# A two-block transformer kernel on one core: a reordered head, ten convolution taps shared with ScalarE, and the second gate computed on VectorE

## What is computed

```
mod_x = silu(c) @ w_ada + b_ada          # 6144 columns: sh1 sc1 g1 sh2 sc2 g2
hx = modulate(rms_norm(x), sh1, sc1);  hc = modulate(rms_norm(ctx), csh1, csc1)
q, k, v, u = split(hx @ w_in);  kc, vc = hc @ w_in[:, 512:1536]
attn = neighbourhood_attention(rope(q), q, rope(k), v, kc, vc, rpb)
a, b = split(u);  h = a * sigmoid(b)
h = depthwise_conv(h, dw_kernel, 31 taps, 512 channels) + dw_bias
conv = silu(layer_norm(h))
x = x + g1 * (concat(attn, conv) @ w_out)
x = x + g2 * (square(relu(modulate(rms_norm(x), sh2, sc2) @ w_mlp1)) @ w_mlp2)
```

## Time and profile before

| | us |
|---|---|
| median of 3 runs | 737.4 |
| lowest and highest | 736.58, 737.42 |
| the profiled execution's own time | 736.31 |
| its span, first to last instruction | 734.5 |
| PE busy | 722.9 (98%) |
| DVE busy | 508.9 (69%) |
| ACT busy | 398.0 (54%) |

### The profile page before, as it was taken

How to read it: one execution, slowest core, us unless ns; L and a number is a source line. 1 busy time by engine, 2 the same in 40 slices (tenths; PEclk the granted TensorE clock), 3 DMA queues, 4 the chain that set the end, 5 groups by cost and what they waited for, 6 DMA issues and landing times.

```text
span 734.5 us, 9784 instructions
## 1 busy us (share of the span) xinstructions
PE 722.9 (98%) x3824; PEld 578.6 (79%) x3824; DVE 508.9 (69%) x924; ACT 398.0 (54%) x662; POOL 25.0 (3%) x44
## 2 busy tenths in 40 slices
PE   8989999999999999999999999999999999999996
PEld 7668885568888888888878777778888888888885
DVE  4678999889667555565988799865857445544544
ACT  3366337886666545556545677666466344334432
POOL 1030012000100000000010000000000000000000
PEclk9999999999999999999999999999999999999999
DMA  9993939945464655445538533344366555655511
GB/s 365 415 354 117 374 112 360 368 161 176 159 223 158 229 192 209 172 163 182 159 101 302 200 115 115 117 176 167 114 230 205 195 175 188 209 175 172 172 58 57
DMA packets 73741, 144.90 MB, mean 197 GB/s; under 512 B 4112, under 2 KB 27664, under 8 KB 72672
## 3 DMA queue, kind: packets, MB, share of 16 engines
q1 hardware_dynamic: 71888, 138.98, 54.6%
q0 software_dynamic: 1520, 5.03, 1.9%
q10 hardware_dynamic: 288, 0.27, 0.1%
HBM read 143.22 MB, written 1.05 MB: 196 GB/s over the span
## 4 chain that ended last, share of the span: by engine, by line
PE 93%; DVE 3%; issue 2%; ACT 1%; POOL 1%; POOLq 0%; DVEq 0%
PE bank L414 22%; PE bank L416 22%; PE bank L415 22%; PE bank L735 5%; PE bank L396 5%; PE bank L733 3%; PE bank L433 2%; PE bank L476 1%; PE bank L454 1%; PE bank L577 1%; PE bank L490 1%; DVE WL L1480 1%; PE bank L599 1%; PE bank L852 1%; PE bank L874 1%
## 5 line engine op out<-in xcount | busy, mean ns | idle before, releaser
L1480 DVE TENSOR_TENSOR WL<-W,WH 128x1024 fp32r<-128x1024 f32 (+2 forms) x222 | 249.5, 1169 | 48.8 <-ACT WH L1005 48.5
L1005 ACT ACTIVATE WH<-W 128x1024 fp32r<-128x1024 f32 (+2 forms) x222 | 211.7, 1011 | 52.9 <-DMA W<-in_w_mlp 40.5
L414 PE MATMUL bank<-WH,AHL 128*128 128x512 f32 (+1 forms) x480 | 189.2, 394 | 2.3 <-DVE WL L1480 2.0
L416 PE MATMUL bank<-WH,AHL 128*128 128x512 f32 (+1 forms) x480 | 185.4, 386 | 0.0
L415 PE MATMUL bank<-WL,AHL 128*128 128x512 f32 (+1 forms) x480 | 185.2, 386 | 0.0
L414 PEld LDWEIGHTS bank<-WH,AHL 128*128 128x128 f32 x480 | 90.2, 188 | 24.0 <-DVE WL L1480 3.5
L416 PEld LDWEIGHTS bank<-WH,AHL 128*128 128x128 f32 x480 | 90.1, 188 | 18.7
L415 PEld LDWEIGHTS bank<-WL,AHL 128*128 128x128 f32 x480 | 90.3, 188 | 16.8
L414 PE MATMUL bank<-WH,HH 128*128 128x512 f32 (+1 forms) x218 | 84.9, 390 | 0.0
L416 PE MATMUL bank<-WH,HL 128*128 128x512 f32 (+1 forms) x218 | 84.5, 388 | 0.0
L415 PE MATMUL bank<-WL,HH 128*128 128x512 f32 (+1 forms) x218 | 84.4, 387 | 0.0
(11 more groups left out here) (265 smaller groups left out, 831.4 us busy)
## 6 DMA issues: line engine op xcount, KB each, us to landing
W<-in_w_mlp SPq DMA_DIRECT2D x32, 1024.0 KB, 5.5
W<-in_w_in SPq DMA_DIRECT2D x24, 1024.0 KB, 5.1
W<-in_w_ada SPq DMA_DIRECT2D x12, 1024.0 KB, 8.0
WX<-in_w_ada SPq DMA_DIRECT2D x12, 1024.0 KB, 9.9
W<-in_w_gate SPq DMA_DIRECT2D x22, 512.0 KB, 4.2
W<-in_w_up SPq DMA_DIRECT2D x22, 512.0 KB, 5.3
W<-in_w_down SPq DMA_DIRECT2D x11, 1024.0 KB, 5.0
W<-in_w_out SPq DMA_DIRECT2D x8, 1024.0 KB, 5.1
```

Of the source, the lines that this page charges most:

```text
L414: e.matmul(po, hs, wh[:, k, c0:c0 + cw], start=first and k == 0, stop=False)
L416: ins = e.matmul(po, ls, wh[:, k, c0:c0 + cw], start=False, stop=last and k == unit.nk - 1)
L1005: e.activation(m.WH[unit.slot][:, c], m.W32[unit.slot][:, c], ACT.Copy).then_inc(S["w_hi"], 1)
L1480: e.tensor_tensor(m.WL[unit.slot][:, c], m.W32[unit.slot][:, c], m.WH[unit.slot][:, c].bitcast(F32), ALU.subtract).then_inc(S["w_lo"], 1)
```

## The change

It reorders the head, moves ten of the thirty-one taps to another form, and takes g2 out of the attention.

1. **Head.** 11 matmuls on ones instead of 16 ahead of `mod_first(0)`, and none instead of 4 ahead of `mod_turn(0)`. The context is loaded two units earlier, ahead of the eighth block's two tiles. ACT squares it after block 5 instead of after block 7, and DVE normalises its first half after block 6 and its second half between the two k units. ACT's table load for the sigmoid moves ahead of block 7, both sigmoids of b behind the k units' WH. Slots 3 and 12 change places in the first 16 entries, so that k's first unit waits for block 5's tile and not for block 6's.
2. **Ten taps.** For taps 21 to 30, ACT writes the product hp * tap into one of two buffers (`tap_products`, 4 instructions of 128x256 for each tap), and DVE adds it to cacc in one instruction of 128x1024 (`add_product`). DVE keeps 80 of its 120 tap instructions; 60 of them and all ten additions stand before the attention. The buffers lie where V and U are, so ACT's copy of V waits for all ten additions.
3. **g2.** Four `w_ada` units of 1 MB, `mod_second` steps 12 to 15, two tails and two of four `rows2_lo` go. Instead SP loads the same 1024x1024 columns as rows in four pieces of 1 MB after the loads of m2 units 2 to 5, DVE sums them over rows (8 instructions of 128x1024) in chunks 2 to 5, ACT and DVE split the sum, and PE adds over partitions with four matmuls of 512 columns (`gate_sum`) in chunk 6.

The core of the diff:

```diff
-    slots = [2, 4, 3, 5, 12, 0, 13, 1, 2, 4, 3, 5, 12, 0, 13, 1, 2, 3, 4, 5, 0, 1]
+    slots = [2, 4, 12, 5, 3, 0, 13, 1, 2, 4, 12, 5, 3, 0, 13, 1, 2, 3, 4, 5, 0, 1]
...
+    def gate_rows(n):                                  # SP
+        w.wait_ge(S["out_mm"], 8)
+        if n > 1:
+            w.wait_ge(S["g2"], 2 * n - 2)
...
-    for n in range(16):
+    for n in range(14):
         load(n)
     e.dma_start(m.XC[:, :, :], ...)
-    for n in range(16, len(units)):
+    for n in range(14, len(units)):
         load(n)
+        if n in gate_at:
+            gate_rows(gate_at.index(n))
...
-    keep_busy(16)                                      # PE
+    keep_busy(11)
     mod_first(0)
-    keep_busy(4)
     mod_turn(0)
     keep_busy(8)
...
+    def gate_sum():
+        w.wait_ge(S["comb_r"], 2)
+        w.wait_ge(S["g2_hi"], 1)
+        w.wait_ge(S["g2"], 9)
+        for n in range(2):
+            cs = slice(512 * n, 512 * n + 512)
+            take(4 + n)
+            e.matmul(bank[4 + n][:, :], m.onesR[:, :].to_broadcast([128, 128]), m.gH[:, cs], start=True, stop=False)
+            e.matmul(bank[4 + n][:, :], m.onesR[:, :].to_broadcast([128, 128]), m.gL[:, cs], start=False,
+                     stop=True).then_inc(S["g2_mm"], 1)
+            frees(4 + n, ("g2", n + 10))
...
-        mod_second(2 * u)                              # PE, attention step u
-        if u:
-            mod_second_tail(u - 1)
+        if u < 4:
+            mod_second(2 * u)
+        if u in (1, 2, 3, 4, 6):
+            mod_second_tail(min(u - 1, 4))
...
-        mod_second(2 * u + 1)
+        mod_second(2 * u + 1 if u < 4 else u + 4)
...
-    for k in range(8):                                 # ACT, head
+    for k in range(6):
         hi()
         high_x(k)
     w.wait_ge(S["l_xc"], 16)
     for tb in range(2):
         square(2 + tb, m.XC[:, tb, :], m.XC2[:, tb, :])
     hi()
+    high_x(6)
     e.activation(m.stat[:, 92:93], m.stat[:, 94:95], ACT.Sigmoid)
+    hi()
+    high_x(7)
+    hi(2)
...
+    def tap_products(*ns):                             # ACT
+        for n in ns:
+            j = 31 - CONV_PRODUCTS + n
+            if n > 1:
+                w.wait_ge(S["conv_add"], n - 1)
+            else:
+                w.wait_ge(S["u_turned" if n == 0 else "c_turned"], (2, 4)[n])
+            for c in range(4):
+                e.activation(m.cprod[n % 2][:, c, :], m.hp[:, c, j:j + 256], ACT.Copy,
+                             scale=m.dw[:, c, j:j + 1]).then_inc(S["conv_prod"], 1)
+    tap_products(0, 1)
     for tb in range(2):
         from_bank("k_mm", 6 + 2 * tb, m.KC[:, tb, :], tb, slice(0, 512), "kc_out")
+        if tb == 0:
+            tap_products(2)
     hi(2)
+    tap_products(3)
     for tb in range(2):
         from_bank("q_mm", 2 + 2 * tb, m.Q[:, tb, :], 2 + tb, slice(0, 512), "q_out", 0.125)
+        tap_products(4 + 2 * tb, 5 + 2 * tb)
...
     for tb in range(2):
         from_bank("v_mm", 2 * tb + 2, m.VC[:, tb, :], 4 + tb, slice(0, 512), "vc_out")
+        tap_products(8 + tb)
     qk_features(0, m.kcT)
     qk_features(1, m.qT)
+    w.wait_ge(S["conv_add"], CONV_PRODUCTS)
     from_bank("v_mm", 6, m.V[:, 0, :], 0, slice(0, 512), "v_out")
...
-    taps(20)                                           # DVE, after rope of K
+    taps(8)
+    add_product()
+    add_product()
+    taps(8)
     lo(2)
+    add_product()
+    taps(4)
+    add_product()
+    w.wait_ge(S["q_out"], 2)
+    rope1(m.QR, m.Q, "rotated")
+    for _ in range(4):
+        taps(6)
+        add_product()
     taps(8)
...
-    taps(52)
+    add_product()
+    add_product()
+    taps(8)
...
-        taps((9, 8, 8, 7, 4, 0, 0, 0)[u])              # DVE, attention step u
+        taps((6, 5, 4, 3, 0, 0, 0, 0)[u])
...
+    def gate_rows(k8):                                 # DVE, twice at the end of chunks 2 to 5
+        rows, ck = m.GW[n % 2][:, k8 % 2, :], m.cs[:, 2 * k8:2 * k8 + 1]
+            fused(m.gacc[:, :], rows, ck, m.gacc[:, :], ALU.mult, ALU.add, "g2")
```

More of the change, by code:

```diff
@@ L80, in __init__ @@
         self.cacc = M("cacc", 72, [128, 4, 256])
+        self.cprod = [M(f"cprod{i}", (68, 56)[i], [128, 4, 256]) for i in range(2)]
         self.ccen = M("ccen", 28, [128, 4, 256])
@@ L100, in __init__ @@
         self.combR = M("combR", 84.75, [128, 1], F32R)
+        self.onesR = M("onesR", 84.8125, [128, 1], F32R)
+        self.GW = [M(f"GW{i}", 60 + 8 * i, [128, 2, D]) for i in range(2)]
+        self.gacc = M("gacc", 76, [128, D])
+        self.gL = M("gL", 76, [128, D], F32R)
+        self.gH = M("gH", 80, [128, D], F32R)
         self.hid = [M(f"hid{i}", 32 + 4 * i, [128, 2, 512]) for i in range(2)]
@@ L472, in keep_busy @@
     def keep_busy(count):
-        w.wait_ge(S["ones"], 1)
+        w.wait_ge(S["fills"], 1)
         for _ in range(count):
@@ L761, in tensor_program @@
         up_wide(c)
-        for tb in range(2):
-            down1(c - 1, tb, False, False)
+        down1(c - 1, 0, False, False)
+        if c == 6:
+            gate_sum()
+        down1(c - 1, 1, False, False)
     up_wide(7)
@@ L1258, in scalar_program @@
         hi(2)
+        if c == 5:
+            w.wait_ge(S["g2"], 8)
+            copy(m.gH[:, :], m.gacc[:, :], "g2_hi")
     hi()
@@ L1574, in vector_program @@
         low_x(k)
-    for tb in range(2):
-        mean_square(2 + tb, (2 + tb,))
-        hat(m.XC, m.XC2, tb, 2 + tb, "c_hat")
-    lo(2)
-    for tb in range(2):
-        w.wait_ge(S["gate_u"], tb + 1)
+        if k == 6:
+            mean_square(2, (2,))
+            hat(m.XC, m.XC2, 0, 2, "c_hat")
+    lo()
+    mean_square(3, (3,))
+    hat(m.XC, m.XC2, 1, 3, "c_hat")
+    lo()
+    for tb in range(2):
+        w.wait_ge(S["gate_sig"], tb + 1)
         w.wait_ge(S["a_mm"], 15 + tb)
@@ L1587, in vector_program @@
     lo(2)
-    conv = {"n": 4}
+    conv = {"n": 4, "added": 0, "last": [0, 0, 0, 0]}
     def taps(count):
@@ L1858, in low_wide, with gate_low, gate_add @@
         tt(flat(m.HL[c % 2][:, ks, :]), m.hid[c % 2][:, p, :], flat(m.HH[c % 2][:, ks, :]).bitcast(F32), ALU.subtract, "hid_lo")
+    def gate_rows(k8):
+        n = k8 // 2
+        w.wait_ge(S[f"l_g{n % 2}"], 16 * (n // 2) + 16)
+        rows, ck = m.GW[n % 2][:, k8 % 2, :], m.cs[:, 2 * k8:2 * k8 + 1]
+        if k8:
+            w.wait_ge(S["g2"], k8)
+            fused(m.gacc[:, :], rows, ck, m.gacc[:, :], ALU.mult, ALU.add, "g2")
+        else:
+            times(m.gacc[:, :], rows, ck, "g2")
+    def gate_low():
+        w.wait_ge(S["g2_hi"], 1)
+        tt(m.gL[:, :], m.gacc[:, :], m.gH[:, :].bitcast(F32), ALU.subtract, "g2")
+    def gate_add():
+        w.wait_ge(S["l_first"], 48)
+        for n in range(2):
+            gv = m.g2b[:, 512 * n:512 * n + 512]
+            w.wait_ge(S["g2_mm"], n + 1)
+            tt(gv, bank[4 + n][:, :], gv, ALU.add, "g2")
     hid_lo(0, 4, 0, 1)
@@ L1873, in vector_program @@
         lo(2)
+        if c < 6:
+            gate_rows(2 * c - 4)
+            gate_rows(2 * c - 3)
+        else:
+            gate_add()
     sum_wide(7, 0)
```

149 lines of the change are left out of this document (81 added, 68 removed).

## The result

The changed kernel takes 741.34 us (median of 5 runs, 740.74 to 743.66) where the kernel before takes 737.4 on the same chip: ratio 1.0066, interval 1.0054 to 1.0078. It is slower by 0.7% (4.9 us by the ratio, 3.9 between the medians). Its profiled execution took 743.66 us, the longest of the five and 2.3 us above their median, with a span of 741.9 and a mean granted clock of 0.990 (before: 0.998). So the profiles stand further apart than the kernels do, and what follows explains the profiles.

A forecast was written before the change was run, and what follows sets the result against it. The prediction took the kernel as bound by TensorE's order, with DVE full before the attention. 7.4 + 0.2 - 2.75 + 1.1 = +5.9 us on the profiled 736.31 gave 742.2, or 743.3 beside the median; range 737.5 to 746.2.

The forecast's parts named there:

- main case: Whole kernel: the summed forecast of 743.3 us, slower, with its own range of 740.3 to 746; chance 0.60.
- Head, -1.9 forecast: End of the head: loading the context earlier removes PE's 2.04 us wait for WL, 1.9 us gained; bounds 0 and 2.5.
- `keep_busy` term: Start of the head: dropping nine `keep_busy` calls changes nothing, taken at 0; bounds -0.8 and +1.
- Ten taps, +7.4 forecast: Ahead of the attention: products and additions start it 7.4 us later, head's 1.9 included; bounds 5.0 and 9.3.
- The second wait of PE that the forecast named: At the first scores: PE waits for ACT, after its wait for kcT; about 8 us in all.
- Clock after the hole, +0.2 forecast: Behind PE's 8 us standstill: PE may restart at a lower clock, 0.2 us; bounds 0 and 2.5.
- listed as a rival: Behind the hole: PE restarts at 1.2 GHz, +2 us, 745.3; chance 0.15 together with a failed head.
- 1.3 to 2.5 worked out by it: Whole sum: by the Trainium skill's restart rule, 1.3 to 2.5 us higher than with a warm clock.
- Attention, -2.75 forecast: Attention: less PE work saves 1.0 us in step 4 and 1.75 in steps 5 to 7; bounds 1.0 and 5.8.
- Gate, +1.1 forecast: Feed forward: four new gate matmuls cost PE 1.1 us, hidden by nothing; bounds 0.9 and 1.3.
- The first rival: Ahead of the attention: hand-over hidden, PE's work decides, -3.6 us, 733.8, or 730.8 with full attention; chance 0.13.

The follow-up runs named there:

- no_products: The changed kernel with all thirty taps on VectorE and no products on ACT, head and gate still changed: 733.34 us, ratio 0.9943 to the kernel before.
- fill_hole: The changed kernel plus 30 `keep_busy` calls between the transposes of Q and KR, so PE works while it would wait: 742.08 us, ratio 1.0062.
- gate_only: The kernel before with only the g2 part of the change, head and taps as before: 734.9 us, ratio 0.9968.
- four_clean: The changed kernel with four product buffers, tenth product behind kcT and qT copies, and both gates' bias-row loads moved into the attention: 739.5 us, ratio 1.0035.
- late_rows: Control: the changed kernel with only the loads of both gates' bias rows moved into the attention: 744.58 us, ratio 1.0109.
- two_later_taps: The changed kernel, two product buffers kept, with eight DVE taps moved from ahead of the attention into its steps 0 to 2: 741.52 us, ratio 1.0060.
- both_undone: The changed kernel without the products, and with 16 and 4 matmuls on ones in the head again: 732.63 us, ratio 0.9937.
- busy_head: The changed kernel with 16 and 4 `keep_busy` calls in the head again, everything else as changed: 742.3 us, ratio 1.0068.

## Why the prediction was right, and where its terms were off

The forecast was 743.3 us, slower, by the hand-over of the products; 741.34 came, in the range of 737.5 to 746.2 and in its main case. The profiled execution was forecast at 742.2 and took 743.66: +7.4 instead of +5.9. The other runs of the change were 1.3 to 2.9 us shorter, so for a typical one the sum was 1 to 2 us too high. The way and the cause were foreseen; that the number came so close is in part luck, because the terms below missed in both directions (head and clock cost 2.3 us more than forecast in the profile, the attention gave 1.0 more).

- **Head, -1.9 forecast.** The WL wait went, as forecast. In the profile of the change k starts at 49.53, only 0.4 us earlier than before. The step that was off is the `keep_busy` term, taken at 0 with a bound of +1, where 1.5 came in this profile: PE waits 1.9 us for the first `w_ada` tile, and the 16 matmuls on ones that took 1.95 us before take 3.11, at a clock of 0.67 from 12 to 15 us. In the profile of no_products they take 1.95, and k starts at 48.0, which is the full 1.9. The term was +1.1 to +1.5 in three profiles of this head and 0 in six, by how long PE waited for the tile. The window from 12 to 15 us, first of the change and then of no_products, and the change's row of the slow matmuls:

```profile
12.00:15.00 3.00, 3.00 (x23) 2.76 (x26) 2.40 (x6) 0.97 (x3) 0.00 (x0) 0.67 1.02 426
```

```profile
12.00:15.00 3.00, 3.00 (x29) 2.07 (x28) 2.05 (x5) 1.57 (x3) 0.00 (x0) 1.00 1.06 444
```

```profile
11.56 3.11 PE L494 MATMUL bank<-ones 128*128 128x128 f32 x16
```

- **Ten taps, +7.4 forecast, +9.9 measured.** The chain ran as written, each hand-over in its place: a product took 1.71 us (1.75 taken), its instructions 500 ns each, and an addition 1.23 (1.25). The groups of both in the kernel after (busy us, mean ns, idle before):

```profile
L1120 ACT ACTIVATE cprod<-hp,vec 128x256 f32<-128x256 f32 x40 | 17.0, 500 | 19.4 <-DVE cacc L1546 19.4
L1546 DVE TENSOR_TENSOR cacc<-cacc,cprod 128x1024 f32<-128x1024 f32 x10 | 12.2, 1225 | 0.9
```

  DVE waited 2.3 us for Q, PE 7.8 us for kcT (8.2). DVE's tenth addition ended 1.6 us later than forecast (114.55 against 112.95), 1.1 of it from the late head, and ACT's qrT 1.5 later. The last 1.0 us is the mis-sized term on the clock, which is counted in the 9.9. The second wait of PE that the forecast named, for ACT at the first scores, did not come: v's first half ended later than ACT's copies.
- **Clock after the hole, +0.2 forecast, +1.0 measured (0.1 to 1.3 in four kernels with the same hole).** The mechanism was listed as a rival and did happen: 0.50 for the first 4 us and more, KR's and QR's transposes at 1.9 us instead of 1.0, v's first half done at 118.2 and not 114.3. The error was to give its 1.4 us of spare time to v's first half alone, when the two sets of transposes ahead of it slow down as well, 1.6 us together from start to start. The forecast took the two levels from the lengths of the matmuls at the start (0.20 and 0.12 us); the profile's granted clock shows 1.00 for that stretch, 2.76 to 9.1 us, so that reading rests on the lengths alone. Behind the hole, lengths and granted clock agree. The section "HAM oscillation" of the page "TensorE: Matmul & The Clock Gate" in the Trainium skill says that a throttled PE pays again at each restart; the trace agrees (0.50), but the price at the first scores was 0.1 to 1.3 us, at most the lower end of the 1.3 to 2.5 worked out by it, since ACT's copies were late too, and fill_hole got no measurable part of it back.
- **Attention, -2.75 forecast, -3.7 measured.** Step 4 gave its 1.0 exactly; steps 5 to 7 gave 2.6 instead of 1.75, 14.8 us against the forecast of 15 to 16. ACT kept up better than assumed: PE waited once for its PT, 0.7 us. The other wait, 0.9 us in step 6 for DVE's bias addition to g1, was not there before and not forecast.
- **Gate, +1.1 forecast.** All that lies behind the attention costs 1.2 us, and no wait over 0.3 us came there. gate_only gives the sign of attention and gate together: -2.75 + 1.1 = -1.65 was forecast, and the ratio of 0.9968 is -2.4 us. The two terms are not separated by a run.
- **What the text did not see.** It put the whole loss on the waits between ACT and DVE, and noted DVE's 5.3 us of extra work ahead of the attention only as part of that chain. With the hand-over mended the loss stays at 0.35% (four_clean), 6.8 us above no_products where the change is 9.1 above it; 1.0 of the 6.8 is the slower normalisation, and moving eight taps takes 5.1 away. The first rival, "the handshake is hidden", would thus not have given 733.8 without moving taps as well.

## What to carry to other kernels

Splitting one accumulation over two engines costs the receiving engine an instruction per part (1.23 us here, against 1.63 for the four taps it replaces) and ties the orders of both together; with two buffers, everything that stands behind the sender's work in its queue waits for the receiver. Ask first where the receiver has idle time: here ten products saved DVE 4 us over the whole kernel, and the same edit put 5 us more in front of a deadline. And when a mended wait brings nothing, look for the next wait at the same place before calling the theory false. Here three delays (the hand-over, DVE's load, and a queue stopped by the experiment) hid one another. Last, read a control's trace and not only its marks: late_rows met the change at two points of time by an early head and a slower instruction that cancelled.

## What was not expected of the hardware

- With the same matmuls on ones in the head, the granted clock from 8 to 12 us differs between profiles: the 16 matmuls behind the first tile took 3.11 us in the change, 2.10 in fill_hole and two_later_taps, and 1.95 in the six others. The three slow ones are those with the longest wait for the tile (1.9 to 2.4 us against 1.0 to 1.7). With the 16 and 4 calls the wait shrinks to 0.2 us or none. The five runs of both_undone lie within 0.52 us, those of no_products within 1.28; of busy_head within 1.49, of the change within 2.92. In gate_only, which has the 16 and 4 calls too, it is 1.47, with a fall of the clock elsewhere.
- The clock can fall where no wait is long. PE had waits of 0.9 and 0.7 us in steps 6 and 7 of the attention. The clock went to about 0.50 there in the profiles of busy_head and gate_only and stayed at 1.00 in the change and the other kernels with the same waits. In busy_head this took back 1.6 us of an advance of 2.5.
- A 128x1024 instruction of VectorE with a scalar operand took 1.80 us instead of 0.76 in the three kernels where GpSimd filled tiles at the same time (likely the cause, not separated). The subtractions for WL, of the same size with two tensors as operands, kept their 1.2 us each beside such fills.
